# Layer norms that scale rows in place and transpose them back, chunks of two tiles for the up phase, and eight output stores

## The reference

```python
x = layer_norm(ALPHA * x + gate1 * jnp.dot(mixed, p['w_out']), p['ln1_g'], p['ln1_b'])
h = x * (1 + scale2) + shift2
up = jnp.dot(h, p['w_up'])                 # 2048 -> 2 * 5504
# ... causal convolution of width 3 over the rows, a and b are the halves of its result
ff = jnp.dot(jax.nn.silu(a) * b, p['w_down'])
y = layer_norm(ALPHA * x + gate2 * ff, p['ln2_g'], p['ln2_b'])
```

## Time and profile before

| | |
|---|---|
| median of 3 runs | 1449.84 us (1448.3 to 1453.35) |
| the profiled execution, its time | 1447.23 us |
| its span, first to last instruction | 1445.6 us |
| PE busy | 1379.4 us, 95% of the span |
| DVE, ACT, POOL busy | 845.4, 570.5, 109.6 us |
| mean granted TensorE clock | 0.981 of full speed |

### The profile page before, as it was taken

One profiled execution on the slowest core, in us unless ns is written; L12 is line 12 of the kernel. 1 busy time (PEld: TensorE's weight loads), 2 busy tenths in 40 slices (PEclk: granted clock), 3 DMA queues, 4 the chain that ended last, 5 costly groups with the idle time before them and its releaser, 6 DMA issues.

```text
span 1445.6 us, 29154 instructions
## 1 busy us (share of the span) xinstructions
PE 1379.4 (95%) x11350; PEld 1305.4 (90%) x11350; DVE 845.4 (58%) x1375; ACT 570.5 (39%) x828; POOL 109.6 (8%) x252
## 2 busy tenths in 40 slices
PE   6999999999898997999999999999999999999992
PEld 5998888898787886998999999999999999999992
DVE  2476546568665447555756554576665545657555
ACT  3523222353532337444444333444444333444333
POOL 1000000014111000001101000010010000101002
PEclk9999999999999999999999999999999999999996
DMA  9999988975676986877454554445445444454521
GB/s 378 379 325 384 351 329 306 339 270 182 226 267 222 349 319 234 310 287 262 141 179 148 182 164 160 162 151 181 160 156 178 161 160 160 163 170 146 197 88 66
DMA packets 89182, 324.86 MB, mean 225 GB/s; under 512 B 10573, under 2 KB 10573, under 8 KB 88720
## 3 DMA queue, kind: packets, MB, share of 16 engines
q1 hardware_dynamic: 81216, 294.69, 57.2%
q0 software_dynamic: 6880, 24.10, 4.8%
q10 hardware_dynamic: 1008, 4.98, 0.9%
HBM read 318.05 MB, written 5.67 MB: 224 GB/s over the span
## 4 chain that ended last, share of the span: by engine, by line
PE 92%; DVE 3%; ACT 2%; DMA 1%; issue 1%; SPq 0%; POOLq 0%; ACTq 0%; POOL 0%; DVEq 0%
PE ps L438 28%; PE ps L440 27%; PE ps L439 27%; PE ps L454 5%; ACT xT L1157 1%; DMA adaY<-w_ada 1%; PE ps L546 1%; PE ps L743 1%; DVE xT L1681 1%; DVE xT L1680 1%; ACT H L1171 1%; DVE wL L1267 1%; PE ps L620 0%; PE ps L667 0%; PE ps L753 0%
## 5 line engine op out<-in xcount | busy, mean ns | idle before, releaser
L1267 DVE TENSOR_TENSOR wL<-raw,wH 128x1024 fp32r<-128x1024 f32 x372 | 448.9, 1217 | 376.4 <-ACT wH L913 373.2
L913 ACT ACTIVATE wH<-raw 128x1024 fp32r<-128x1024 f32 x372 | 389.5, 1053 | 596.7 <-PE ps L440 572.5
L438 PE MATMUL ps<-hL,wH 128*128 128x288 f32 x2016 | 603.6, 299 | 7.0 <-DVE hL L1305 4.0
L440 PE MATMUL ps<-hH,wH 128*128 128x288 f32 x2016 | 600.2, 298 | 0.0
L439 PE MATMUL ps<-hH,wL 128*128 128x288 f32 x2016 | 599.0, 297 | 0.0
L438 PEld LDWEIGHTS ps<-hL,wH 128*128 128x128 f32 x2016 | 382.1, 190 | 20.3 <-issue 8.9
L439 PEld LDWEIGHTS ps<-hH,wL 128*128 128x128 f32 x2016 | 381.3, 189 | 0.5 <-issue 0.5
L440 PEld LDWEIGHTS ps<-hH,wH 128*128 128x128 f32 x2016 | 380.1, 189 | 0.0
L438 PE MATMUL ps<-ffL,wH 128*128 128x288 f32 x688 | 204.4, 297 | 0.0
L439 PE MATMUL ps<-ffH,wL 128*128 128x288 f32 x688 | 203.0, 295 | 0.0
L440 PE MATMUL ps<-ffH,wH 128*128 128x288 f32 x688 | 202.3, 294 | 0.0
(11 more groups left out here) (227 smaller groups left out, 982.3 us busy)
## 6 DMA issues: line engine op xcount, KB each, us to landing
raw<-w_up SPq DMA_DIRECT2D x168, 512.0 KB, 3.5
ada<-w_ada SPq DMA_DIRECT2D x112, 512.0 KB, 6.3
raw<-w_down SPq DMA_DIRECT2D x84, 512.0 KB, 3.5
raw<-w_in SPq DMA_DIRECT2D x80, 512.0 KB, 7.8
adaX<-w_ada SPq DMA_DIRECT2D x40, 512.0 KB, 5.4
adaY<-w_ada SPq DMA_DIRECT2D x40, 512.0 KB, 7.3
raw<-w_out SPq DMA_DIRECT2D x32, 512.0 KB, 4.9
KV<-keys POOLq DMA_DIRECT2D x16, 512.0 KB, 5.7
```

The costliest lines, as they stand in the source:

```text
L438: nc.tensor.matmul(out, wH[:, w:w + P], rhs_lo(kk), start=start, stop=False)
L440: mm = nc.tensor.matmul(out, wH[:, w:w + P], rhs_hi(kk), start=False, stop=stop)
L913: nc.scalar.activation(wH[:, o:o + cols], raw[:, o:o + cols], ACT.Copy).then_inc(hi_done, 1)
L1267: vec_tt(wL[:, o:o + cols], raw[:, o:o + cols], wH[:, o:o + cols].bitcast(F32), ALU.subtract).then_inc(split_done, 1)
```

## The change

- ACT now copies the transposed rows from PSUM into row buffers in SBUF (`copy_rows`: 256 and 32 rows of 2048 features). `bn_stats` reads these. The copy of `S4` to `xT` is gone, as are DG, `spread_rows`, `RN` and `centre`. Copies and statistics of the groups 0 to 2 stand one to three steps later in the program than before.
- `scale_rows(ln, c)`: DVE scales and shifts two tiles' features of all rows, in place, with one `tensor_scalar` for each of the three row blocks (128 x 256, 128 x 256, 32 x 256).
- `turn_back(ln, c, banks)`: PE transposes the two tiles back into PSUM, three transposes a tile, one bank a tile. In the first norm three banks (4, 5, 7) take turns, so tile k can be written when `affine` has read tile k-3.
- First norm: eight chunks of two tiles. ACT reads PSUM for the prompt's h and for `affine`; DVE reads PSUM for the samples, and ACT waits for that (`samples_read`) before it reads. From chunk 3 on ACT does `hi` of slab c+1 behind the chunk, and DVE `lo` of it. On PE chunk 0 is turned back behind the modulation slabs 8 to 11, chunk 1 behind 12 to 15, and chunk j+2 behind slab j of the up phase. `ada_turn` now stands behind slab 0.
- Second norm: DVE scales all eight chunks, PE turns them into eight banks, ACT applies gain and shift to 13 tiles and DVE to 3. POOL has no part. SP issues eight stores of two tiles.
- The first 32 slabs of the up phase are written out instead of looped.

The engines in parts of the diff follow each other as PE, SP, ACT, DVE. Left out are semaphore names, the places of buffers, loop bookkeeping, and removed lines that the printed kernel shows.

```diff
-            def spread_rows(ln):
-
-                pe.wait_ge(diag_ready, ln + 1)
-                for j in range(2):
-                    b = take(pe, ("ln", ln, j), 4 + j)
+            def turn_back(ln, c, banks):
+
+                pe.wait_ge(xn_ready, 8 * ln + c + 1)
+                for k in (2 * c, 2 * c + 1):
+                    b = take(pe, ("back", ln, k), banks[k % len(banks)])
                     for r in range(3):
                         n = P if r < 2 else SAMP
-                        mm = nc.tensor.matmul(b[:, r * P:r * P + n], ones[0:n, :], DG[0:n, (2 * r + j) * P:(2 * r + j) * P + n],
-                                              start=True, stop=True)
-                    fill(mm, ("ln", ln, j))
+                        mm = nc.tensor.transpose(b[:, r * P:r * P + n], row_block(ln, r, k * P, (k + 1) * P), ident[0:n, 0:n])
+                    fill(mm, ("back", ln, k))
...
-            for k in range(8, 16):
+            for k in range(8, 12):
                 ada_next(a + k)
-            ada_turn(U_SC2B, ("turn", U_SC2B))
...
+            turn_back(0, 0, (4, 5, 7))
+            for k in range(12, 16):
+                ada_next(a + k)
+            turn_back(0, 1, (4, 5, 7))
+
+            def behind_first(j):
+
+                if j == 0:
+                    ada_turn(U_SC2B, ("turn", U_SC2B), bank=6)
+                if j + 2 < 8:
+                    turn_back(0, j + 2, (4, 5, 7))
...
                 for j in range(n):
-                    pe.wait_ge(h2_ready, (j * deep + deep - 1) // 4 + 1)
+                    pe.wait_ge(h2_ready, (j * deep + deep - 1) // 2 + 1)
                     products(s + j, i0 + j, lambda kk: tile(hH, deep * j + kk), lambda kk: tile(hL, deep * j + kk),
                              banks, j == 0, j == n - 1, ktiles=deep, taking=lambda t: take(pe, (job, banks[t]), banks[t], it, per))
+                    if behind is not None:
+                        behind(j)
...
+                    up_group(S_UP[0], 0, ("up", 0, "a"), 0, 2, units=0, behind=behind_first)
...
-                    spread_rows(1)
+                    for c in range(8):
+                        turn_back(1, c, (0, 1, 2, 3, 4, 5, 6, 7))
...
+            for c in range(8):
+                released(sp, ("back", 1, 2 * c))
+                released(sp, ("back", 1, 2 * c + 1))
+                sp.dma_start(io["yT"][:, c * 2 * ROWS:(c + 1) * 2 * ROWS], xT[:, c * 2 * ROWS:(c + 1) * 2 * ROWS]).then_inc(stored, 16)
+            sp.wait_ge(stored, 16 * 8)
...
+                        if g and j == 2:
+                            copy_rows(g - 1, 0)
                         if S_OUT + 16 + 4 * g + j in TURN_AT:
                             unit_copy(TURN_AT[S_OUT + 16 + 4 * g + j])
-                        if g and j == 1:
-                            copy_sum(g - 1, 0)
...
+
+            def copy_rows(g, ln):
+
+                for r in range(3):
+                    n = P if r < 2 else SAMP
+                    b = filled(act, ("rows", ln, g, r))
+                    release(nc.scalar.activation(row_block(ln, r, g * 512, (g + 1) * 512), b[0:n, :], ACT.Copy), ("rows", ln, g, r))
...
+            deviation(0)
+            for c in range(8):
+                if c >= 2:
+                    act.wait_ge(h2_ready, c - 1)
+                act.wait_ge(samples_read, c + 1)
+                for t in range(2):
+                    k = 2 * c + t
+                    s, o = (SC2 + k) * MODS, (SH2 + k) * MODS
+                    b = filled(act, ("back", 0, k))
+                    y = nc.scalar.activation(tile(H2, 2 * (c % 2) + t, 0, SEQ), b[:, 0:SEQ], ACT.Identity, scale=modT[:, s:s + 1], bias=modT[:, o:o + 1])
+                y.then_inc(h2_prompt, 1)
+                act.wait_ge(h2_prompt, c + 1)
+                act.wait_ge(h2_32, c + 1)
+                nc.scalar.activation(tiles(hH, 2 * c, 2), tiles(H2, 2 * (c % 2), 2), ACT.Copy).then_inc(h2H, 1)
+                for t in range(2):
+                    release(affine(0, 2 * c + t), ("back", 0, 2 * c + t))
+                if c == 1:
                     unit_copy(U_SC2B)
...
+                if c >= 3:
+                    hi_ahead(S_UP[0], S_UP[0] // 4, c - 2)
...
+                            if u or i > 5:
+                                hi_ahead(u * 16 + s0, u * 4 + s0 // 4, i)
...
-                            if g and j == 0:
-                                copy_sum(g - 1, 1)
-            affine = normalise(1, V_G2, V_B2)
...
-                act.dma_start(io["yT"][:, b4 * 4 * ROWS:(b4 + 1) * 4 * ROWS], xT[:, b4 * 4 * ROWS:(b4 + 1) * 4 * ROWS]).then_inc(stored, 16)
-            act.wait_ge(stored, 16 * 4)
+                            if g and j == 3:
+                                copy_rows(g - 1, 1)
+            deviation(1)
+            for k in range(KT):
+                if k < 10 or k % 2 == 0:
+                    release(affine(1, k), ("back", 1, k))
...
             def row_statistics(g, ln):
                 for r in range(3):
                     n, job = P if r < 2 else SAMP, ("rows", ln, g, r)
-                    b = filled(dve, job)
-                    release(nc.vector.bn_stats(small[0:n, 50 + 24 * r + 6 * g:56 + 24 * r + 6 * g], b[0:n, :]), job)
+                    released(dve, job)
+                    ins = nc.vector.bn_stats(small[0:n, 50 + 24 * r + 6 * g:56 + 24 * r + 6 * g], row_block(ln, r, g * 512, (g + 1) * 512))
+                return ins
...
+
+            def scale_rows(ln, c):
+
                 for r in range(3):
...
+                    x = row_block(ln, r, c * 256, (c + 1) * 256)
+                    ins = vec_ts(x, x, small[0:n, 142 + r:143 + r], small[0:n, 145 + r:146 + r], ALU.mult, ALU.add)
+                ins.then_inc(xn_ready, 1)
...
-                    if g and j == 2:
+                    if g and j == 3:
                         row_statistics(g - 1, 0)
...
-            centre(0, 0)
...
+            for c in range(3):
+                scale_rows(0, c)
+            for c in range(8):
+                samples = by_seq(tiles(H2, 2 * (c % 2), 2, SEQ, ROWS), 2)
+                for t in range(2):
+                    k = 2 * c + t
+                    b = filled(dve, ("back", 0, k))
+                    ins = vec_tt(samples[:, t:t + 1], by_seq(b[:, SEQ:ROWS].rearrange("p (k c) -> p k c", k=1), 1), mods(SC2 + k, 1)[1], ALU.mult)
+                ins.then_inc(samples_read, 1)
+                dve.wait_ge(samples_read, c + 1)
+                vec_tt(samples, samples, mods(SH2 + 2 * c, 2)[1], ALU.add).then_inc(h2_32, 1)
+                if c + 3 < 8:
+                    scale_rows(0, c + 3)
+                if c == 2:
                     unit_finish(U_SC2B)
-                dve.wait_ge(h2H, b4 + 1)
-                vec_tt(tiles(hL, 4 * b4, 4), tiles(H2, 0, 4), tiles(hH, 4 * b4, 4).bitcast(F32), ALU.subtract).then_inc(h2_ready, 1)
+                dve.wait_ge(h2H, c + 1)
+                vec_tt(tiles(hL, 2 * c, 2), tiles(H2, 2 * (c % 2), 2), tiles(hH, 2 * c, 2).bitcast(F32), ALU.subtract).then_inc(h2_ready, 1)
+                if c >= 3:
+                    lo(S_UP[0] + c - 2 + AHEAD, (c - 2 + AHEAD) % RING)
...
-                            if g and j == 3:
+                            if g and j == 4:
                                 row_statistics(g - 1, 1)
             normalise(1)
-            for b4 in range(3):
-                centre(b4, 1)
+            for c in range(8):
+                scale_rows(1, c)
+            for k in (11, 13, 15):
+                b = filled(dve, ("back", 1, k))
+                release(vec_ts(tile(xT, k), b[:, 0:ROWS], vec[:, V_G2 + k:V_G2 + k + 1], vec[:, V_B2 + k:V_B2 + k + 1], ALU.mult, ALU.add), ("back", 1, k))
...
```

More of the change, by code:

```diff
@@ L1142, in _, with deviation @@
             out_rest()
[L1144 to L1145 removed]
+            def deviation(ln):
+                copy_rows(3, ln)
                 act.wait_ge(ln_var, ln + 1)
[L1147 to L1160 removed]
@@ L1205, in _ @@
                 if ph == 0:
-                    with act.Fori(0, 2) as u:
+                    for u in range(2):
                         for i in range(1, 17):
@@ L1636, in residual @@
                 if ln or g:
-                    dve.wait_ge(s4_copied, 4 * ln + g)
+                    for r in range(3):
+                        filled(dve, ("rows", ln, g - 1, r) if g else ("rows", 0, 3, r))
                 for t in range(4):
@@ L1768, in _ @@
                 if ph == 0:
-                    with dve.Fori(0, 2) as u:
-                        steps.enter(u, 9)
+                    for u in range(2):
                         for i in range(1, 17):
```

122 lines of the change are left out of this document (30 added, 92 removed).

## The result

The changed kernel takes 1446.79 us (median of 19 runs, 1442.16 to 1449.88), the kernel before 1450.25 (19 runs, 1448.3 to 1453.83): a ratio of 0.997, 95% interval 0.9962 to 0.9978. It is faster by 0.3%, some 4 us. Forecast were 8.9 us less and a range of 1435 to 1446.5; the direction is right, the gain is less than half of it. The profiled execution took 1446.01, its span is 1444.3 (before: 1447.23 and 1445.6).

What follows compares the result with a forecast made beforehand. PE was taken to bound the kernel (92% of the chain), with gains only in its waits or slow stretches and the tail. First norm +3.3, down phase +0.3, tail -12.5 sum to -8.9: median 1440.9, range 1435 to 1446.5.

Steps and rivals of the forecast that it cites:

- Part 1: Start of the up phase: last modulation slab lands by bandwidth at 556.3, so slab 0 begins at 557.5 instead of 559.08.
- Parts 2 and 3: First norm, slabs 0 to 7: slab 2 from 566.0, then chunks limit PE; slab 8 at 596.3, 3.3 later than 593.00.
- The ring: First norm from chunk 3: chunks pass one by one through ACT and DVE, 5.5 each, against PE's 3.9 a slab.
- six transposes 0.66: First norm: PE turns back a chunk of two tiles in 0.66, at 0.11 a transpose.
- I count the clock as full throughout: First norm: no clock fall assumed; one fall while PE is the slower side would cost 1.5.
- Part 4: Moved statistics: covered by a modulation burst in the output projection; 0.15 shows twice in the down phase, 0.3 lost.
- Part 5: Tail: transposes begin at 1420.8, PE ends them at 1429.9, end at 1433.1; 12.5 saved, bounds 15.2 and 7.6.
- The factor of 1.73: Tail: L753's twelve took 3.50 there and 2.02 in the first norm; scales a transpose from 0.11 to 0.19.
- The upper bound: Tail: transposes at L753's spacing of 0.29 take 14.0, ending at 1434.8; the tail then saves 7.6.
- the tail's transposes are dear: Rival, chance 0.15: at 0.29 each the tail saves 7.6, net -4.0; 1445.8 to 1449.8, no change that can be told.
- the first norm costs nothing: Rival, chance 0.12: shorter ACT PSUM reads and slack gain 1.3 in the first norm; 1433.6 to 1436.3.
- The half clock in the new pauses: Slower rival, chance 0.05: PE waits before slabs 5 to 7 lower the clock; if it stayed, 27 lost, at 1464.

Runs made afterwards that it cites:

- the two runs with the earlier sum: Changed kernel with the previous group's statistics behind the residual: 1444.08; and that plus paired 32-row transposes, later DVE split and idle products ahead of the tail's transposes: 1436.26.
- pairs alone: Changed kernel with each chunk's transposes reordered, four of 128 rows and then the two of 32: 1441.36 us, ratio 0.9943 to the kernel before.
- pairs and the later split: Changed kernel with grouped 32-row transposes, DVE's split behind the next samples, idle products ahead of the tail's transposes, statistics behind the residual: 1436.26 us, ratio 0.9906.
- full sample rows: Changed kernel with the tail's 32 sample rows transposed as if they were 128: 1440.62 us, measured once.
- the kernel without its part: Kernel before with only the second norm changed, first norm and loops as before: 1442.62 us, ratio 0.9951.

## Why the prediction was wrong

**Part 1: right mechanism, a little too early.** Slab 0 came at 558.58 instead of 557.5: the last modulation slab was used at 556.92 instead of 556.3, and the six transposes behind it, with slab 0's first product, cost 1.1 instead of 0.66. The transfer opened the phase, as the two runs with the earlier sum showed.

**Parts 2 and 3: the right end, partly by luck, and one term mis-sized.** Slab 8 came at 596.55 against 596.3. But the stretch had begun 1.6 late, for which the forecast had nothing, and the slabs 0 to 7 took 37.97 where it had 38.8. The ring is there: a period of 5.19 (5.5), chunk 4's samples at 572.78 (571.5), chunk 7 ready at 591.24 (591.2). It was said to cost 4.6 over PE's own work (596.3 less 591.7). It costs 1.04: the term "six transposes 0.66" measured 1.13, 2.8 more in six chunks, so PE was late by itself and only slab 7 had to wait. That slower PE hid the ring, which the forecast took for the whole loss. Both had to go together: pairs alone turned into waits, pairs and the later split gained 2.8.

"I count the clock as full throughout" held in this profile and not in all. Two runs with the same first norm, those with 15 idle products and with full sample rows, had a clock of 0.50 for some 10 us, from ahead of slab 0 until 568 and 565.5; their slab 8 came 58.5 and 58.0 behind the burst instead of 54.5. So the changed first norm costs more in some executions than this pair of profiles shows.

**Part 4:** some 0.6 in the down phase instead of 0.3. DVE's first wait of 1.29 became none, as forecast, and the residual came 0.4 and 0.3 later in groups 1 and 2.

**Part 5 failed, and with it the forecast.** The step is "a transpose takes 0.19 ... I take the middle value, since the 0.11 that I scale is from transposes of the same form". They are not: `turn_rows` takes 128 rows in every weight load, `turn_back` 32 in each third one. What a tile costs at the low clock is 0.86 (0.53 of loads and a gap of 0.33) instead of 0.57, so 13.8 instead of 9.1, and that 4.7 is all but 0.2 of what the tail lacked. Two errors are in it. The factor of 1.73 was too small even for one form: full transposes stand 0.213 apart at 0.50, which gives 0.64 a tile where the forecast had 0.57: some 1.1 of the 4.7. The change from 128 to 32 rows explains the other 3.5, the step from 0.64 to 0.86. A smaller term was wrong as well, without showing: DVE's scaling took 7.83 instead of 6.5, hidden behind PE.

The upper bound, L753's own spacing of 0.29, came out to the digit, and that is in part luck. L753's weight loads have the same two shapes in the same proportion, and the same kind of gap:

```profile
1421.78 1.49 PEld L753 LDWEIGHTS ps<-DG,ones 32*128 32x128 f32 x6 [0.22 <-issue]
```

But these are plain fp32 products, four with 128 rows and then two with 32 in each bank, with one gap of 0.22 in six, where the transposes have one of 0.33 in three. That the two mixes have the same mean nobody could know; that the row held the dear shape, and the row that was scaled didn't, could be seen. So the bounds and the rival "the tail's transposes are dear" were right: a tail saving of 7.6 and 1445.8 to 1449.8 in all. It had 0.15, which was too little.

The Trainium skill ("TensorE: Matmul & The Clock Gate", Part 4: PE-mode transpose) has about 275 ns for a transpose in a kernel, and speaks of it as a duration. The trace agrees with it as a duration: at full clock a transpose of `turn_rows` lasts 0.27. But the next one starts 0.11 behind it, and the prediction misread the figure when it multiplied it by 48. That the tail's mean of 288 is near it says nothing: it is made of transposes 0.213 apart and of gaps. The same section of the Trainium skill says that transposes don't count as activity for the full clock, and that isn't borne out here: they held 1.00 for 8.8 us behind idle products, gaps of 0.17 and all, and in the run with full sample rows they brought 0.50 back to 1.00. With the 32-row loads they didn't bring it back in 13.8 us.

**Not in the forecast at all:** the spacing of 0.1344, 2.8 of the profiled execution. What sets it is open, and so is whether the change has a part in it; it makes the profile pair look worse (-1.3) than the medians (-3.5).

**The other rivals.** That the first norm costs nothing fell: slabs 0 to 7 took 37.97 for 33.92, and the kernel without its part is some 3 faster. The half clock in the new pauses of the up phase fell too: in the profiles of the changed kernel and of its variants the granted clock was 1.00 from slab 2 to slab 8, the waits of 1.04 among them. Where it fell, in six of nine, it did so ahead of slab 0, among waits for transfers, and in four of them it lasted into slab 0.

## What to carry to other kernels

A weight load of 32 rows behind loads of 128 came with a gap of 0.17 between loads (0.33 at the lower clock): group such matmuls, or fill them up to 128 rows where the buffer allows. When an unmeasured operation is bounded by two rows, compare their shapes one by one, row counts of the weights too; a row that lacks one of the shapes is no price for the mix, and the range must reach the one that has it. Keep apart how long a matmul lasts and how far apart two start: only the second is a price. And ahead of a tail on PE, look at the pause in front of it: 30 products whose results nobody reads took 5 us off the tail here, more than the whole change gained.

## What the runs showed of the hardware

- With no idle products (a pause of PE of 4.07) and with 15 (2.07) the granted clock fell to 0.50 ahead of the tail's transposes or within 1.6 of their start, and with the 32-row transposes it stayed there; with 30 (a pause of 0.1) it stayed at 1.00. A pause of 2.53 ahead of matmuls of 288 columns was followed by no fall.
- fp32 transposes of 128 rows and columns start 0.11 apart at a granted clock of 1.00 and 0.213 apart at 0.50; one lasts 0.27 and 0.42.
- Ahead of a weight load of 32 rows behind one of 128 there was a gap of 0.17 (0.33 at 0.50) between loads, and none between two loads of 32 rows. Transposing the 32 rows side by side took the tail's 48 from 13.83 to 11.22, transposing them as 128 rows to 7.66.
- Transposes of full row count brought the granted clock from 0.50 to 1.00 some 4 us behind their start; with each third of 32 rows and gaps they ran 13.8 us at 0.50.
- In five of 13 profiles products of the same code stood 0.1344 apart in one or both of two phases, otherwise 0.1333, at a granted clock of 1.00 in both cases. What sets it stays open.
- Eight stores of 288 KB within 4.9 us filled the DMA (389 GB/s): the last took 3.2 from issue to landing, where it took 2.5 with the same stores spread over 6.4 us.
